# Routed experts taken in a mixed order of their sizes, computed on chip, in a diffusion block with mixture of experts

## What is computed

```python
s = sigmoid(x @ w_router)                       # 2048 x 64
_, eidx = top_k(where(gmask > 0, s + b_router, -inf), 6)
gates = sel / sum(sel) * 2.5
# each routed expert e: its tokens in blocks of 128
y = swiglu(x[tok], w1[e], w3[e], w2[e]) * gate  # 1024 -> 256 -> 1024
routed = segment_sum(y, tok)
shared = swiglu(x, ws1, ws3, ws2)               # all 2048 tokens
out = rmsnorm(x + g2 * (routed + shared), norm_final)
```

## Time and profile before

| | us |
|---|---|
| three runs | 2813.97, 2810.34, 2804.68 (median 2810.34) |
| the profiled execution | 2836.76, its span 2835.0 |
| stage `experts`, first to last block's start on PE | 1220.6 to 2757.4 of the span |
| of it, shared blocks 0 to 15 | 1220.6 to 1371.4 |
| routed blocks 16 to 143 | 1371.4 to 2690.6 |
| routed blocks 144 to 150 (of the last expert) | 2690.6 to 2757.4 |

### The profile page before, as it was taken

The page is one execution under the profiler, slowest core; times in us unless marked ns, Lnnn a source line. Parts: engine busy times, 40 slices in busy tenths (PEclk is TensorE's granted clock), DMA queues, the critical chain, the costliest instruction groups (busy, mean ns, idle before and its releaser), DMA issues. The chain is left out here.

```text
span 2835.0 us, 51166 instructions
## 1 busy us (share of the span) xinstructions
PE 2541.6 (90%) x11957; PEld 2031.0 (72%) x11958; DVE 1733.6 (61%) x2714; ACT 1014.7 (36%) x1615; POOL 991.8 (35%) x1006
## 2 busy tenths in 40 slices
PE   7999999999849889669999999999998999999990
PEld 4787777777638777558777777777776788777780
DVE  4664564574236666664775775775589745686643
ACT  3212444323212222132442453543356422454422
POOL 1210035602245665521233433433333333343334
PEclk9999999999969998889999999999999999999995
DMA  7865768574456555255897887997789966698757
GB/s 276 312 256 200 266 229 307 198 277 163 163 211 227 167 167 167 86 162 124 280 291 207 238 258 222 292 276 212 193 262 356 301 186 155 165 341 267 211 107 270
DMA packets 239095, 641.38 MB, mean 226 GB/s; under 512 B 24108, under 2 KB 37744, under 8 KB 223536
## 3 DMA queue, kind: packets, MB, share of 16 engines
q1 hardware_dynamic: 188736, 459.72, 45.4%
q0 software_dynamic: 50288, 180.75, 26.0%
HBM read 463.06 MB, written 177.33 MB: 226 GB/s over the span
## 5 line engine op out<-in xcount | busy, mean ns | idle before, releaser
L2043 POOL DMA_INDIRECT sum_d<-w_shared_raw,give x136 | 235.7, 1733 | 786.6 <-DVE w_shared_raw L2185 560.2
L2143 DVE TENSOR_TENSOR w_exp_lo<-w_exp,w_exp_hi (+1 forms) x256 | 307.5, 1221 | 86.2 <-ACT w_exp_hi L2082 68.8
L2289 PE MATMUL ps_h<-w_exp_hi,x_exp_t_hi 128*128 (+1 forms) x1216 | 315.2, 402 | 31.6 <-ACT w_exp_hi L2082 25.8
L2082 ACT ACTIVATE w_exp_hi<-w_exp (+1 forms) x256 | 260.8, 1056 | 191.6 <-DMA w_exp<-in_experts 106.6
L2289 PE MATMUL ps_h<-w_exp_hi,x_exp_t_lo 128*128 (+1 forms) x1216 | 321.7, 406 | 0.0
L2289 PE MATMUL ps_h<-w_exp_lo,x_exp_t_hi 128*128 (+1 forms) x1216 | 311.1, 398 | 0.0
L2289 PEld LDWEIGHTS ps_h<-w_exp_hi,x_exp_t_hi 128*128 128x128 f32 x1216 | 229.2, 190 | 93.8 <-ACT w_exp_hi L2082 21.3
L1134 PE MATMUL ps_p<-wa_hi,hx_split 128*128 128x512 f32 x1088 | 278.0, 401 | 4.3 <-DVE kvqg_out L100 3.3
L2289 PEld LDWEIGHTS ps_h<-w_exp_lo,x_exp_t_hi 128*128 128x128 f32 x1216 | 230.3, 189 | 56.5
L2108 ACT ACTIVATE h_exp_t_hi<-ps_ht 128x256 fp32r<-128x256 f32 x152 | 58.1, 383 | 531.3 <-PE ps_ht L2298 510.7
L2289 PEld LDWEIGHTS ps_h<-w_exp_hi,x_exp_t_lo 128*128 128x128 f32 x1216 | 217.7, 189 | 41.4
(11 more groups left out here) (276 smaller groups left out, 4396.4 us busy)
## 6 DMA issues: line engine op xcount, KB each, us to landing
w_exp<-in_experts SPq DMA_DIRECT2D x386, 512.0 KB
hx_split<-hx_d SPq DMA_DIRECT2D x54, 1024.0 KB, 6.0
rec_m<-rec_d SPq DMA_DIRECT2D x16, 1536.0 KB, 7.5
hx_d<-hx_split SPq DMA_DIRECT2D x18, 1024.0 KB, 7.0
wm_rest<-in_w_mod_rest POOLq DMA_DIRECT2D x16, 1024.0 KB, 6.1
rec_d<-kvqg_out SPq DMA_DIRECT2D x48, 256.0 KB, 4.2
xt<-in_xt POOLq DMA_DIRECT2D x18, 512.0 KB, 8.8
rec_d<-kt_kvf_out SPq DMA_DIRECT2D x32, 256.0 KB, 4.9
```

The costliest lines, as they stand in the source:

```text
L2043: pool.indirect_dma_start(sum_d[:, :], bass.IndirectOffsetOnAxis(give[:, par:par + 1], 0), y[:, par], None, compute_op=ALU.add).then_inc(a ...
L2082: act.activation(w[0][:, piece(e, i)].bitcast(F32R), raw(e, i), ACT.Copy).then_inc(gu_hi, 1)
L2143: dve.tensor_tensor(w[1][:, piece(e, i)].bitcast(F32R), raw(e, i), w[0][:, piece(e, i)], ALU.subtract).then_inc(gu_lo, 1)
L2289: last = pe.matmul(out, x[:, j * P:(j + 1) * P].bitcast(F32R), w_part[:, bass.ds(w_at + j * stride, 512)].bitcast(F32R), start=(start and ...
```

## The change

Experts are ranked by their number of blocks (ties by index, the larger first), and position p of the order takes the rank whose number is p with its six bits reversed: 0, 32, 16, 48, 8, ... `sizes` (new, DVE, after block 2) computes the ranks with comparisons; a matmul of 128x128 on PE after block 3 (with the matrix of ones, `R.order[:, 1]`) turns them into two rows, blocks and expert number of each position; `counts` then follows after block 4, `columns` (four operations longer) after block 5, PE's row matmuls after block 6, the copy of the table after block 7. POOL fetches the lists after block 5's add. A further constant, `rank_at`, is loaded at the start of `mixer_out`.

Since 41 of 64 experts have one block, the order of sizes, by position, becomes

8 1 3 1 4 1 2 1 7 1 2 1 3 1 1 1 7 1 2 1 3 1 1 1 5 1 2 1 3 1 1 1 7 1 2 1 4 1 1 1 6 1 2 1 3 1 1 1 7 1 2 1 3 1 1 1 5 1 2 1 3 1 1 1

SP now reads which weights to load from a row (`expert_at`), once per expert. The first routed expert is known only with the table: its weights are loaded after shared tile 11 instead of at the start, and split in block 12 (`FIRST_SPLIT`) instead of block 0.

```diff
@@ experts
+    FIRST_SPLIT = NT - 4
...
         def change(eng, k):
             if isinstance(k, int) and k <= NT:
-                return expert_of(eng, k) + 1, k in (0, NT)
+                return expert_of(eng, k) + 1, k in (FIRST_SPLIT, NT)
...
+            def expert_at(e):
+                return sp.value_load(ends_row[0:1, bass.ds(e, 1)], min_val=0, max_val=NE - 1)
...
             def load_free(e, slot):
+                row = expert_at(e)
                 for i in range(N_GU):
                     sp.wait_ge(gu_lo, (e - RING) * N_GU + i + 1)
-                    load(e, slot, i)
+                    load(row, slot, i)
...
             for k in range(2, STAGES):
                 load_shared(k)
-            for i in range(N_GU + N_D):
-                load(1, 1, i)
             for k in range(STAGES, NT):
                 sp.wait_ge(xt_lo, (k - STAGES + 1) * 2)
                 load_shared(k)
+                if k == 11:
+                    table(sp)
+                    row = expert_at(1)
+                    for i in range(N_GU + N_D):
+                        load(row, 1, i)
...
-            for k in range(1, 4):
+            for k in range(1, 6):
                 add(k)
...
+            def sizes(tabs):
...
+                tabs.of(dve.scalar_tensor_tensor(key[:], nt[:, 1:NE], float(N_EXP), R.iota[:], ALU.mult, ALU.subtract))
+                tabs.of(dve.tensor_tensor(own_key[:], key[:], ident[:, 0:N_EXP], ALU.mult))
+                tabs.of(dve.tensor_reduce(kc[:], own_key[:], AX.X, ALU.add))
+                tabs.of(dve.tensor_tensor(own_key[:], nt[:, 1:NE], ident[:, 0:N_EXP], ALU.mult))
+                tabs.of(dve.tensor_reduce(ncol[:], own_key[:], AX.X, ALU.add))
+                tabs.of(dve.tensor_scalar(own_key[:], key[:], kc[:], None, ALU.is_gt))
+                tabs.of(dve.tensor_reduce(rnk[:], own_key[:], AX.X, ALU.add))
+                dve.tensor_scalar(by_size[:, 0], R.rank_at[:], rnk[:], ncol[:], ALU.is_equal, ALU.mult).then_inc(sized, 1)
+                dve.tensor_scalar(by_size[:, 1], R.rank_at[:], rnk[:], R.kcol[:, 2:3], ALU.is_equal, ALU.mult).then_inc(sized, 1)
...
-                if k == 4:
+                if k == 3:
+                    pe.wait_ge(sized, 2)
+                    pe.wait_ge(R.carry_done, NT)
+                    pe.matmul(ps_r[:, 0:2 * N_EXP], R.order[:, 1], by_size.rearrange("p a e -> p (a e)"),
+                              start=True, stop=True).then_inc(ordered, 1)
+                if k == 6:
                     pe.wait_ge(bcol_done, 2)
```

More of the change, by code:

```diff
@@ L1202, in __init__ @@
         self.iota = sb("iota_s", [P, N_EXP])
[L1203 removed]
+        self.kcol = sb("kcol_s", [P, 3])
+        self.rank_at = sb("rank_at_s", [P, N_EXP])
         self.token = sb("token_s", [P, NT], U32)
@@ L1816, in constants @@
     out["list_base"] = (out["iota"] + 1) * 2048
-    out["kcol"] = np.stack([i, i + P], 1).astype(np.float32)
+    out["kcol"] = np.stack([i, i + P, i + 1], 1).astype(np.float32)
+    out["rank_at"] = np.repeat(np.array([[int(f"{p:06b}"[::-1], 2) for p in range(64)]], np.float32), P, 0)
     out["token"] = (np.arange(16)[None] * P + np.arange(P)[:, None]).astype(np.uint32)
@@ L1869, in experts @@
         cmpn = sb("cmp_nt", [P, 2, NE])
+        room, spare = R.prod[:].rearrange("p j e -> p (j e)"), R.eq6[:].rearrange("p b j e -> p (b j e)")[:, 4 * P:6 * P]
+        key, own_key = spare[:, 0:N_EXP], spare[:, N_EXP:2 * N_EXP]
+        by_size = room[:, 0:2 * N_EXP].rearrange("p (a e) -> p a e", a=2)
+        cmpe = room[:, 2 * N_EXP:2 * N_EXP + 2 * NE].rearrange("p (c e) -> p c e", c=2)
+        kc = sb("size_key_col", [P, 1])
+        ncol = sb("nt_col", [P, 1])
+        rnk = sb("size_rank", [P, 1])
+        er = sb("expert_row", [P, NE + 1])
+        de = sb("expert_steps", [P, NE])
+        ecol = sb("expert_cols", [P, 2])
         bcol = sb("block_cols", [P, 2, 2])
@@ L1973, in load_free @@
             def load_free(e, slot):
+                row = expert_at(e)
                 for i in range(N_GU):
                     sp.wait_ge(gu_lo, (e - RING) * N_GU + i + 1)
-                    load(e, slot, i)
+                    load(row, slot, i)
                 for i in range(N_D):
                     sp.wait_ge(wd_lo, (e - RING) * N_D + i + 1)
-                    load(e, slot, N_GU + i)
+                    load(row, slot, N_GU + i)
             for k in range(2):
@@ L1991, in _ @@
                 load_shared(k)
+                if k == 11:
[3 more added lines that the diff above has]
+                        load(row, 1, i)
+            row = expert_at(2)
             sp.wait_ge(xt_lo, NT * 2)
             for i in range(N_GU):
-                load(2, 0, i)
+                load(row, 0, i)
             sp.wait_ge(wd_lo, N_D)
             for i in range(N_GU, N_GU + N_D):
-                load(2, 0, i)
+                load(row, 0, i)
             load_free(3, 1)
@@ L2044, in scatter @@
                                         y[:, par], None, compute_op=ALU.add).then_inc(added, 16)
-            for k in range(4, 11):
+            for k in range(6, 11):
                 add(k)
@@ L2238, in columns @@
                     dve.tensor_scalar(bcol[:, c, 0:1], bcol[:, c, 0:1], float(NE - 1), None, ALU.min).then_inc(bcol_done, 1)
-                dve.tensor_copy(ends_row[:, 0:NE], end[0:1, :]).then_inc(rows_done, 1)
+                dve.tensor_copy(ends_row[:, 0:NE], er[0:1, 0:NE]).then_inc(rows_done, 1)
                 dve.tensor_scalar(ends_row[:, NE:NE + 1], end[0:1, NE - 1:NE], float(-NT), None, ALU.add).then_inc(rows_done, 1)
-            tabs = []
+            tabs = Count(dve, tab_own)
             def after(k):
@@ L2249, in after @@
                 if k == 2:
-                    tabs.append(counts())
-                if k == 3:
-                    columns(tabs[0])
+                    sizes(tabs)
+                if k == 4:
+                    counts(tabs)
+                if k == 5:
+                    columns(tabs)
                 if k == 8:
```

23 lines of the change are left out of this document (14 added, 9 removed).

## The result

The changed kernel takes 2824.4 us (median of 8 runs, 2819.2 to 2831.4); the kernel before, run beside it on the same chip, 2811.4. The ratio is 1.005, with a 95% interval of 1.0032 to 1.0067: some 13 us slower, where 1 us slower was forecast as the likeliest. The time lies in the whole range that was given (2790 to 2832), but above the forecast's own (2804 to 2820). So the change costs between nothing and 0.5%, and why it isn't the same each time is part of the answer.

A forecast was written before the change was run, and what follows sets the result against it. PE was taken as bound by waiting at full clock, with 98.1 us lost in 128 routed blocks. +5.6 - 5.7 + 0.4 + 0.4 + 0.1 + 0.5 = +1.3 on 2810.3 gave 2811.6, say 2812; range 2790 to 2832.

The forecast's parts named there:

- the signs named: Shared block 1 within 10 us, shared part 4 to 6 shorter, 136 routed blocks about 1391, gather waits some 45.
- The order, +5.6 us: Routed part: the new order's groups, priced from earlier windows, lose 103.7 us against 98.1; ends -13 to +29.
- (1, 2, 1, n): Routed part: eight groups of experts with these block counts, n of 3 or more, each priced at 7.3 us lost.
- the window 1, 2, 1, 2, 5: Routed part of the earlier trace: 11 blocks in 112.2 us against 104.9, 7.3 lost, taken as a group's price.
- The start of the shared part, -5.7 us: Shared block 0: without the first routed expert's pieces, its down product and all later shared blocks come 5.7 us earlier.
- The row matmuls and `columns`: Shared part, table building: 0.4 us for one more PE matmul group and 0.4 us for four more DVE operations.
- The late split: Shared block 12: splitting the first routed expert's weights there runs over into block 13, 0.1 us, 0 to 1.
- The constant: Start of the mixer: one more DMA in SP's row delays the first `w_out` rows, +0.5 us.
- SP's register loads: SP's weight loading: one register load per expert, between nothing and 1 us, hidden by SP's idle time, taken as 0.
- the last single experts: End of the routed part: three single-block experts lose 1.5 us, since no loads follow them.
- The slower one: Routed part: a second burst meets the first's remainder; groups lose 9 us, rows of three 7.5; 2835 us, chance 0.27.
- Late gathers become rare: Routed part: half of the gathers in time gives 2782 us, all 2752; chance 0.18.

The follow-up runs named there:

- e1: The changed kernel with experts in index order again, its table, row reads and late load kept: 2810.7 us, ratio 0.9998.
- e2: The kernel before with only the late load and split of the first routed expert's weights added: 2808.8 us, ratio 0.9990.
- e3: The changed kernel with POOL issuing the gather of block k+3 ahead of the scatter of block k-1: 2759.2 us, ratio 0.9823.
- e5: The changed kernel with SP issuing the next expert's gate and up pieces ahead of the current one's down pieces: 2803.1 us, ratio 0.9873.
- e11: The changed kernel, unaltered, compared a second time with the kernel before: 2843.0 us, ratio 1.0009.
- e4: The kernel before with POOL issuing the gather of block k+3 ahead of the scatter of block k-1: 2774.5 us, ratio 0.9871.

## Why the time came out slower than forecast

The direction and the wide range were right, the size wasn't: +1.3 us was forecast, and the three comparisons give +0.5%, +0.1% and +0.4%, some 9.5 us in the mean. Of the signs named, block 1 came within 10 us and the waits moved as said (gathers up, `h_exp_t_lo` down); but the routed part took 1405.9, 1391.6 and 1402.2 us instead of about 1391 (of its 135 blocks, not 136), and the shared part was 3.2 us shorter instead of 4 to 6.

**The order, +5.6 us, is the term that failed.** Over three traces of the changed kernel it lost 118.0, 103.7 and 114.3 us, 112.0 in the mean; over three in index order with the same queues (before, e1, e2) 98.0, 98.5 and 98.7, 98.4 in the mean. The order costs 13.6 us, not 5.6. Taken apart:

| | mixed, three traces | index, three traces |
|---|---|---|
| lost | 118.0, 103.7, 114.3 | 98.0, 98.5, 98.7 |
| down matmuls behind a drop, beyond 3.1 us | 17.8, 7.6, 15.4 | 2.9, 6.5, 6.4 |
| the rest | 100.2, 96.1, 98.9 | 95.1, 92.0, 92.3 |

The rest differs by 98.4 - 93.1 = 5.3 us, close to the forecast. But the second line is the least that the clock cost: the eight transposes ahead of those twelve matmuls are often slowed too (1.51 us for 1.09 above). From the start of the transposes to the end of the twelve, the drops cost 20.8, 9.6 and 18.0 us in the mixed order and 2.9, 7.2 and 7.1 in index order, 10.4 us more in the mean, and then the rest differs by 3.2. The prices of the groups hold at full clock. (1, 2, 1, n) was priced at 7.3 and lost 8.8, 7.6 and 8.7, and without what follows a drop 7.2, 6.8 and 7.2; (1, n) was priced at 4.1 and lost 5.2, 3.6 and 3.8 (4.1, 3.6 and 3.8 without); (1, 1, 1, n), at 5.9, lost 6.0, 5.8 and 6.1. The eight groups (1, 2, 1, n) alone lost 8 x 1.1 = 8.6 us more than their price, which is about the whole miss of this term. Where they lost it is the clock: a late gather of 2 us takes PE's clock down about every second time, and the mixed order has more of them (29 against 22 in the mean) and longer ones (1.8 us against 1.5).

The step that failed is thus the price of 7.3 us for a group (1, 2, 1, n), read in the earlier trace rows; the three traces have 8.4 in the mean. I took the window 1, 2, 1, 2, 5 at a clock of 1.00 as the price of the pattern, and the one window of 0.96 beside it only as an argument of a rival. But the window at 1.00 was a lucky sample of something that varies. The same eleven blocks in index order in e1 (first row) and e2 (second), each from its trace:

```profile
1622.40:1736.30 113.90, 108.34 (x507) 86.66 (x506) 76.14 (x107) 48.70 (x74) 37.43 (x44) 0.99 0.84 244
```

```profile
1616.50:1730.30 113.80, 108.41 (x507) 86.67 (x506) 76.23 (x107) 48.73 (x74) 37.44 (x44) 0.99 0.84 244
```

They lose 9.0 and 8.9 us at 0.99 where the earlier trace rows had 112.2 - 104.9 = 7.3 at 1.00. With a price of 9.0 the sum would have come to 117, and the forecast to +15.

**The start of the shared part, -5.7 us: right to the point where I stopped.** Block 1 starts 9.93 us after block 0 (within 10 had been said), and the down product of block 0 starts 18.2 us after it, against 18.1 forecast and 23.8 before: 5.6 us earlier. Then this, after:

```profile
1205.57 2.11 PE L2335 MATMUL ps_h<-w_exp_hi,x_exp_t_hi 128*128 128x512 f32 x8 [1.60 <-ACT x_exp_t_hi L2117]
...
1213.82 0.73 PE L2335 MATMUL ps_y<-w_exp_hi,h_exp_t_hi 128*128 128x512 f32 x2 [2.18 <-DVE h_exp_t_lo L2187]
1214.39 0.79 PE L2335 MATMUL ps_y<-w_exp_lo,h_exp_t_hi 128*128 128x512 f32 x2
1214.98 1.06 PE L2335 MATMUL ps_y<-w_exp_hi,h_exp_t_lo 128*128 128x512 f32 x2
...
1218.63 2.12 PE L2335 MATMUL ps_h<-w_exp_hi,x_exp_t_hi 128*128 128x512 f32 x8
```

Part of the down matmuls come at 1.06 us a pair instead of 0.63, and block 2 starts 4.8 us behind the down product instead of 3.3: 1.5 us are given back, again by the clock behind an idle time of PE (the wait itself was there before too, with 1.90 us and no longer matmul behind it). That leaves -4.0 for blocks 0 and 1.

**The small terms.** The row matmuls and `columns`, forecast at +0.8 us together, are seen as block 6 with 10.27 us where block 4 had 9.71 before, +0.6, and block 3 with 8.78 against 8.66, +0.1. So the shared part is 3.2 us shorter, where -4.8 had been forecast. The late split cost nothing (block 12 takes 8.65 us; 0.1 had been forecast). The constant delays `w_out` by 0.5 us: POOL waits 17.02 us for it instead of 16.52, as forecast. Whether these 0.5 us reach the end of the kernel isn't shown, beside differences of 25 us in the same stage. SP's register loads cost nothing that shows: e1 has them, and loses 98.5 us in the routed part against 98.0.

**One place was overlooked**, at the very end. With a single-block expert last, its down pieces are split in the last block, where nothing hides them:

```profile
2758.26 2.35 DVE L2172 TENSOR_TENSOR w_exp_lo<-w_exp,w_exp_hi  x2
2760.52 1.40 DVE L2209 SCALAR_TENSOR_TENSOR w_shared_raw<-ps_y,gate,g_row 128x512 f32<-128x512 f32 x2
2761.84 0.41 DVE L2187 TENSOR_TENSOR h_exp_t_lo<-ps_ht,h_exp_t_hi 128x256 fp32r<-128x256 f32 x1
...
2762.66 1.22 PE L2335 MATMUL ps_y<-w_exp_hi,h_exp_t_hi 128*128 x2 [3.80 <-DVE h_exp_t_lo L2187]
```

From the start of block 151 to PE's last matmul it is 19.1 us, before 15.1, and 2.2 us of these 4.0 reach the end of the kernel. The wait of 3.80 us is followed by the fallen clock here too: the twelve down matmuls take 5.4 us instead of 3.1. All kernels with a single-block expert last have 18.1 to 19.2 us there, all in index order (an 8 last) 15.1 to 16.6. I had priced the last single experts by their loads, of which there are none, and not by their splits.

**The sum with what was measured**: 13.6 (order) - 3.2 (shared part) + 2.2 (last block) + 0.5 (constant) = +13.1 us, of which the 0.5 is argued. The misses of the larger terms all point the same way, so nothing in the sum was saved by errors that cancel. That it equals the +13 of the first comparison is chance: the order's 13.6 is a mean of three traces each, and the mean of the three comparisons is nearer +9.5. The first pair of traces alone would give 20.0 - 3.2 + 2.2 + 0.5 = +19.5.

**The rivals.** The slower one came true in its size (it asked for groups at 9 us and for a gather's clock cost) but not in its mechanism: it held that the second burst meets what is left of the first. There are still two late gathers in a group (1, 2, 1, n), as before, and the rows of three, which it put at 7.5 us, stayed at 6.0. It was the clock, which it named last and in passing. "Late gathers become rare" was wrong for this kernel, and right as a statement of what there is to win: its 2752 us is close to e3's 2759. By the rule of the Trainium skill that the prediction weighed ("DMA: Bandwidth & Descriptors", queues taken in turn packet by packet) a gather beside a full queue would hardly be waited for. The traces don't agree for every case, and e5 shows that it depends on the burst: with eight pieces started together gathers made PE wait for up to 3.4 us (in e11), with the same pieces spread for 1.3 at most.

The longer the wait, the more often the clock falls (numbers below). What stays open is why an idle time of the same length sometimes takes it down and sometimes doesn't, and so why one comparison of the changed kernel gave no difference and two gave 0.4 to 0.5%.

## What to carry to other kernels

An order of work units is as good or bad as the queues let it be: here the same order costs 14 us in the routed part (5 to 20 by the trace) or gains 9 to 20 there, and moving one small gather ahead of a scatter in its queue was worth more than any order: 38 us in index order (e4), some 60 in the mixed one (e3 against the changed kernel, by their ratios). When a price is read from a window, read the same pattern in as many windows and executions as there are, and look at the granted clock of each; the one with a clock below 1.00 is part of the price, not an outlier. And a unit that is short at the end of the program has its preparation uncovered.

## What the hardware did that I had not expected

In the 14 traces of this case there are 201 late gathers in the routed part, each followed by the same twelve matmuls. Of the 94 with less than 1.5 us of PE idle, one comes with a clock drop; of the 107 with 1.5 us or more, 50: 11 of 40 below 2.0 us, 29 of 55 from 2.0 to 2.5, 10 of 12 above. Such a drop costs some 1.2 us more in those twelve matmuls alone (40.8 us over 34 in the three traces of the changed kernel), 1.4 us with the transposes ahead of them, in a stretch in which PE is busy for some 95% of the time. It needs no gather: in the 14 routed parts the granted clock falls 55 times, 51 times at these late gathers and four times behind another wait of PE of 2.0 to 2.8 us. In e4, which has no late gather, it looks the same behind DVE:

```profile
1371.93 1.22 PE L2290 MATMUL ps_y<-w_exp_hi,h_exp_t_hi 128*128 x2 [2.77 <-DVE h_exp_t_lo L2164]
1372.94 1.05 PE L2290 MATMUL ps_y<-w_exp_lo,h_exp_t_hi 128*128 x2
1373.80 1.05 PE L2290 MATMUL ps_y<-w_exp_hi,h_exp_t_lo 128*128 x2
```

The Trainium skill ("TensorE: Matmul & The Clock Gate", Part 1) says that PE's clock is set by how busy PE has been. The traces agree that it falls behind idle time (granted clock 0.81 in the 8.8 us around the late gather above), and add that a single wait of some 2 us in a dense stream is enough about half of the time, so that a wait on PE can cost half as much again as its row says, or more.

A gather of 128 rows that is issued in the same 10 us as eight 512 KB pieces takes 9.9 us, where the median of the changed kernel's gathers is 6.5; issued one block earlier it is never awaited (e3, e4), though the DMA engines are then busier (share 0.86 against 0.82).
